# Two chained transformer blocks: in the second pass of the last projection, TensorE takes nine matmuls of one output bank ahead of the last weight chunk

## What is computed

```python
def swiglu_ffn(h, w_ffn_in, w_ffn_out):
    gate, up = jnp.split(h @ w_ffn_in, 2, axis=-1)
    return (jax.nn.silu(gate) * up) @ w_ffn_out        # [512, 2816] @ [2816, 1024]

y = swiglu_ffn(h, w_ffn_in[l], w_ffn_out[l])
x = x + ga2 * rmsnorm(y, post_ffn_g[l])                # the output, [512, 1024]
```

## Time and profile before

| | us |
|---|---|
| median of three runs | 1335.21 (1334.09 to 1336.07) |
| the profiled execution | 1334.96 |
| its span in the profile | 1333.2 |
| TensorE matmuls busy in the span | 1313.8 (99%) |
| VectorE busy | 982.8 (74%) |
| ScalarE busy | 554.2 (42%) |
| GpSimd busy | 88.2 (7%) |

### The profile page before, as it was taken

How to read it: one execution, slowest core, us unless ns; L and a number is a source line. 1 busy time by engine, 2 the same in 40 slices (tenths; PEclk the granted TensorE clock), 3 DMA queues, 4 the chain that set the end, 5 groups by cost and what they waited for, 6 DMA issues and landing times.

```text
span 1333.2 us, 15857 instructions
## 1 busy us (share of the span) xinstructions
PE 1313.8 (99%) x6443; PEld 1065.8 (80%) x6443; DVE 982.8 (74%) x1218; ACT 554.2 (42%) x770; POOL 88.2 (7%) x153
## 2 busy tenths in 40 slices
PE   7999999999999999999999999999999999999997
PEld 4799688888888888888888777778878888888885
DVE  4787877999778777677759799866795444346988
ACT  4553444344333343222332566774443222224543
POOL 0000000000001000100000011000002210000001
PEclk9999999999999999999999999999999999999999
DMA  9544055325455546654222211122204333325565
GB/s 387 199 133 137 2 172 199 129 87 187 158 174 179 182 162 207 222 201 164 92 99 95 95 64 48 49 95 95 95 32 158 117 120 103 104 103 195 189 221 190
DMA packets 34473, 188.03 MB, mean 141 GB/s; under 512 B 4304, under 2 KB 5088, under 8 KB 18016
## 3 DMA queue, kind: packets, MB, share of 16 engines
q1 hardware_dynamic: 20976, 140.32, 29.7%
q0 software_dynamic: 13424, 46.69, 10.8%
HBM read 182.79 MB, written 4.20 MB: 140 GB/s over the span
## 4 chain that ended last, share of the span: by engine, by line
PE 84%; DVE 8%; ACT 3%; DMA 3%; issue 2%; SPq 0%; DVEq 0%; ACTq 0%
PE bank L1695 25%; PE bank L1697 24%; PE bank L1696 24%; DVE WL L947 2%; PE bank L2039 2%; PE bank L2040 2%; PE bank L2045 2%; DMA raw<-weights 1%; DMA adaf<-ada 1%; PE bank L1900 1%; DVE ada_acc L989 1%; PE bank L2235 1%; ACT WH L448 1%; PE bank L2205 1%; DVE raw L960 1%
## 5 line engine op out<-in xcount | busy, mean ns | idle before, releaser
L1695 PE MATMUL bank<-hH,WH 128*128 128x512 f32 x992 | 390.1, 393 | 0.9 <-DVE WL L947 0.5
L1697 PE MATMUL bank<-hH,WL 128*128 128x512 f32 x992 | 386.4, 390 | 0.0
L1696 PE MATMUL bank<-hL,WH 128*128 128x512 f32 x992 | 386.3, 389 | 0.0
L947 DVE TENSOR_TENSOR WL<-raw,WH 128x2048 fp32r<-128x2048 f32 (+1 forms) x114 | 253.6, 2227 | 153.8 <-ACT WH L448 153.7
L448 ACT ACTIVATE WH<-raw 128x2048 fp32r<-128x2048 f32 (+1 forms) x117 | 218.0, 1866 | 237.1 <-DMA raw<-weights 179.5
L1695 PEld LDWEIGHTS bank<-hH,WH 128*128 128x128 f32 x992 | 186.3, 188 | 42.5 <-issue 3.3
L1697 PEld LDWEIGHTS bank<-hH,WL 128*128 128x128 f32 x992 | 186.2, 188 | 39.4
L1696 PEld LDWEIGHTS bank<-hL,WH 128*128 128x128 f32 x992 | 186.4, 188 | 37.7 <-issue 0.2
L989 DVE SCALAR_TENSOR_TENSOR ada_acc<-ada_half,csil,ada_acc 128x1024 f32<-128x1024 f32 x70 | 89.7, 1281 | 4.9 <-DMA ada_half<-ada_later 2.3
L1444 DVE SCALAR_TENSOR_TENSOR cacc<-uT,vec,cacc 128x511 f32<-128x511 f32 (+29 forms) x120 | 83.3, 756 | 0.0
L401 POOL DMA_DIRECT2D ada_half<-ada_later x80 | 42.6, 532 | 569.7 <-DVE ada_acc L989 334.9
(11 more groups left out here) (360 smaller groups left out, 2176.8 us busy)
## 6 DMA issues: line engine op xcount, KB each, us to landing
raw<-weights SPq DMA_DIRECT2D x119, 1024.0 KB, 5.0
ada_half<-ada_later POOLq DMA_DIRECT2D x80, 512.0 KB, 4.5
adaf<-ada SPq DMA_DIRECT2D x8, 1024.0 KB, 19.8
xT<-x_t SPq DMA_DIRECT2D x4, 512.0 KB, 6.0
x_rows<-xB POOLq DMA_DIRECT2D x32, 64.0 KB, 2.2
gF<-x_rows POOLq DMA_DIRECT2D x3, 512.0 KB, 6.9
ctxT<-ctx_t SPq DMA_DIRECT2D x1, 1024.0 KB, 28.0
out_t<-gF SPq DMA_DIRECT2D x2, 512.0 KB, 2.6
```

What stands on the lines that cost most here:

```text
L947: TT_(lo_of(c, 0, width), raw_of(c, 0, width), hi_of(c, 0, width), sub).then_inc(s.lo_done, 1)
L1695: mm(o, lh, rh, start=start, stop=False, skip_group_check=skip)
L1696: mm(o, lh, rl, start=False, stop=False, skip_group_check=skip)
L1697: return mm(o, ll, rh, start=False, stop=stop, skip_group_check=skip)
```

## The change

Nine matmuls, `row2` with x = 0 for q = 7, 8 and 9, are taken ahead of the wait for the last chunk. No operation is added or removed, no wait is changed.

```diff
+            for q in range(PAIRED - 4, PAIRED - 1):
+                row2(q, (0,))
             q = PAIRED - 1
             have(C_REST + q)
             for x in range(2):
                 product(C_REST + q, q, 1, 4, W_A21, 4, (x,), False, True).then_inc(s.y_done, 1)
             for x in range(2):
                 product(C_REST + q, q, 0, 4, W_A11, 2, (x,), False, True).then_inc(s.y_done, 1)
-            for x in range(2):
-                for q in range(PAIRED - 4, PAIRED):
-                    ins = row2(q, (x,), q == PAIRED - 1)
-                ins.then_inc(s.y_done, 1)
+            row2(q, (0,), True).then_inc(s.y_done, 1)
+            for q in range(PAIRED - 4, PAIRED):
+                ins = row2(q, (1,), q == PAIRED - 1)
+            ins.then_inc(s.y_done, 1)
```

## The result

Over 22 runs of each kernel the median went from 1334.69 to 1336.48 us: the ratio is 1.0012, with a 95% interval of 1.0007 to 1.0018, some 1.6 us (0.9 to 2.4); the medians themselves are 1.79 us apart. The kernel is a little slower, and by less than the 2.67 us that the prediction took as no change.

The account below looks back on a forecast made before the run. VectorE was taken as the bound in the tail. Its one term, +1.72 us, on the profiled 1334.96 us gave 1336.68 us, and on the runs' median the forecast 1336.9 us; range 1335.2 to 1338.2 us.

Parts of the forecast that it names:

- The place of the wait: TensorE's 1.36 us idle time in the tail is the wait for the tenth chunk, not the last.
- The count of 48 matmuls: Behind TensorE's idle time stand 48 matmuls: 12 each for bank 7, bank 6, the last chunk and the tenth chunk.
- The rival in which the nine fill a wait for the last chunk: At TensorE's 1.36 us idle time: closings only 0.36 us late, 1335.6 us; chance 3%.
- VectorE as the bound: In the tail, any stop of VectorE between 1318.61 and 1330.16 goes to the end in full.
- Every step of the list: VectorE's tail: L1670 1.56 and 1.64 us late, L1673 on bank 2 1.72 us, no more waiting for banks 3, 6, 7.
- The term: VectorE's delay at L1673 on bank 2: closing 2.04 us later, less 0.32 us to spare, +1.72 us at the end.
- The bounds given for the sum: VectorE's delay on bank 2 lies between 1.58 and 2.04 us, hanging on the 0.53 us from closing matmul to VectorE's start.
- The end on TensorE: In the tail, VectorE's stop is made good before bank 7 comes; time stays at 1335.2 us; chance 6%.
- The clock: TensorE's clock falls to 1.2 GHz behind its idle time; for all 48 matmuls 10.9 us more, 1345.5 us; chance 3%.
- The gap ahead of L1657: VectorE's gap of some 0.1 us, for a root from ScalarE, stays and gives nothing back.

Follow-up runs that it names:

- the six: Against the kernel before, six matmuls of bank 6 (q = 7 and 8) go ahead of the wait for the tenth chunk, into TensorE's idle time; ratio 0.9998.
- the eighteen: Against the changed kernel, the nine bank 7 matmuls for q = 7 to 9 also go ahead of the last chunk; 1338.13 us, ratio 1.0027 to before.
- the first version: Against the kernel before, six bank 6 matmuls in TensorE's idle time, banks 4 and 5 closed earlier, L1667 and L1682 on GpSimd; ratio 0.9999.

## Why the prediction was right

**The place of the wait.** The count of 48 matmuls held: the idle time belongs to the tenth chunk and stayed (1.36 and 1.41 us). The rival in which the nine fill a wait for the last chunk is out, and the six that were really put into an idle time gained nothing either.

**VectorE as the bound.** Every step of the list moved as it was worked out, counted from the pair of low parts: the first L1670 by 1.46 us (expected 1.56), the first L1673 by 1.62 (1.72), the second by 1.64, L1657 and the last pair by 1.63. There were no more waits for banks 3, 6 and 7.

**The size.** The term was 0.1 us too large, in the one number that was taken from elsewhere: 0.53 us from a closing matmul's start to VectorE's, read in the up projection. In the tail it is 0.43, and 0.42 to 0.43 in every other run in which VectorE waits for a bank; why it is 0.1 us less than in the up projection no run shows. The bounds given for the sum, 1.58 to 2.04 us, hold 1.63. The time forecast, 1336.9 us, lies 0.4 us above the 1336.48 measured, and that is the starting level: the median of before was 1335.21 us over three runs and 1334.69 over 22. That the level came out so near is in part luck.

**The end on TensorE** (first rival) fell with the eighteen and with the six. The Trainium skill's rule that stood beside it, from "Perfetto Trace Analysis", section "Identifying the Most-Contended Engine", names the engine with the highest occupancy, here TensorE with 98% to 99% of the span. In the tail the runs go against it: with the six, TensorE is 1.27 us earlier and the tail only 0.02 us shorter. Whether it holds for the rest of the kernel no run here tests.

**The clock** (third rival) did not fall. Busy time and granted clock of the changed kernel over the stretch of the earlier trace rows, the clock being the 1.00 ahead of the last two numbers; from 1313.10 to 1324.40, with all 48 matmuls in it, it is 1.00 too:

```profile
1314.20:1325.50 11.30, 10.19 (x45) 8.07 (x44) 9.71 (x18) 4.33 (x14) 2.54 (x2) 1.00 0.03 11
```

**The gap ahead of L1657** was told of as some 0.1 us that gives nothing back, and VectorE as waiting for nothing in the tail. It is a wait of some 0.18 us for the root (0.24 us from L1647 to L1657 in place of 0.06). For the change that is right, since ScalarE's chain moves with bank 2. As a general statement it is not: with bank 2 on time it gave back 0.19 us.

## What to carry to other kernels

An engine that is busy 99% of the time need not set the end of the kernel, when another has to finish what it leaves; compare, step by step, when each result is closed with when its reader gets to it, and put work that nobody waits for behind the closings and not ahead of them. Work moved ahead of a wait can help only if the engine stands still at that very wait: count instructions back from the end to find whose wait an idle time is. Before giving work to GpSimd, look at what VectorE does at that moment.

## What the runs showed of the hardware

- **GpSimd and VectorE hold each other up, one instruction at a time.** In the first version the two GpSimd products of the same shape took 1.26 and 2.24 us. Its rows by tile (line, engine, operation, count: shortest, median and longest duration in ns, first and last start):

```profile
L439 POOL TENSOR_TENSOR gained<-parts,gpB x2: 1257/1747/2237, 1323.6 to 1325.8; 128x512 f32<-128x512 f32 x2
```

  The long one began at 1323.55, inside VectorE's sum of two SBUF operands (1323.39 to 1324.66), and took 0.98 us longer than the other; the next began as that one ended, and now VectorE's sum, begun 0.04 us later, took 2.27 us in place of 1.28. The five runs with L1667 on GpSimd show the first case again: the first of its products began beside the second of VectorE's low parts, which has two SBUF operands too, and took 1.59 to 2.76 us. The longest is in the run on the changed kernel, where of four products only the first lay beside the low parts:

```profile
L435 POOL TENSOR_TENSOR gained<-parts,gpB x4: 1280/1298/2762, 1313.6 to 1321.4; 128x512 f32<-128x512 f32 x4
```

  Each of these six long products ended 1.13 to 1.15 us behind the end of VectorE's instruction, whenever it had begun. Beside VectorE instructions that read a PSUM bank, GpSimd's products took 1.29 us each (2.55 us for the two) and VectorE's rows kept their 0.68 us. The Trainium skill states this, in "SBUF — State Buffer", section "SBUF: two separate sides": a VectorE instruction with two SBUF inputs and a GpSimd one that reads SBUF take turns on a shared port, and who comes first keeps it for the whole instruction. The trace agrees to 0.1 or 0.2 us: if the second had begun only at the end of the first, it would have ended 1.26 to 1.29 us behind it, and it ended 1.05 to 1.15 us behind it.
- **TensorE's lead over VectorE differs from execution to execution.** The idle time ahead of the tenth chunk was 0.56 to 1.41 us in the profiles of the seven kernels that leave that part as it was. The tenth chunk's first matmul, counted from VectorE's pair of low parts, came at 1.80 or 1.81 us in all of them, since the low part sets it. A filling that is sized to one profile's idle time can be too large in the next.
